# A two-layer diffusion trunk: vectors on ScalarE's queue, inputs loaded first, and the first projection's four jobs in two half passes

## The reference

```python
silu_c = jax.nn.silu(c)
sh1, sc1, g1, sh2, sc2, g2 = jnp.split((silu_c @ ada_w[i] + ada_b[i])[:, None, :], 6, axis=-1)
hl = modulate(rms_norm(x, norm1_g[i]), sh1, sc1)      # h * (1 + scale) + shift
q, k, v = jnp.split(h @ w_qkv, 3, axis=-1)            # w_qkv is 1024 x 3072
```

## Time and profile before

| | |
|---|---|
| median of 3 runs | 1165.8 us (1165.01 to 1168.77) |
| span of the profiled execution | 1166.4 us (no other time is given for it) |
| mean granted TensorE clock | 0.943 of full |
| TensorE busy | 983.8 us, 84% of the span |
| VectorE, ScalarE, GpSimd busy | 402.4, 365.3, 218.6 us |
| DMA | 321.76 MB, mean 276 GB/s |
| chain that ended last, by engine | PE 66%, DMA 18%, DVE 6%, issue 4%, ACT 3% |

### The profile page before, as it was taken

One profiled execution on the slowest core, in us unless ns is written; L12 is line 12 of the kernel. 1 busy time (PEld: TensorE's weight loads), 2 busy tenths in 40 slices (PEclk: granted clock), 3 DMA queues, 4 the chain that ended last, 5 costly groups with the idle time before them and its releaser, 6 DMA issues.

```text
span 1166.4 us, 24481 instructions
## 1 busy us (share of the span) xinstructions
PE 983.8 (84%) x9634; PEld 662.7 (57%) x9635; DVE 402.4 (34%) x848; ACT 365.3 (31%) x777; POOL 218.6 (19%) x329
## 2 busy tenths in 40 slices
PE   4899999988899979799898659999999768996571
PEld 1577777544555655466566447887555644664340
DVE  1533331346733522122122283122853621221113
ACT  3532222466832222122222344233751211120101
POOL 0000000000000034244344201910000132442221
PEclk9899999999999999899999879999999898998895
DMA  9766655998230759999999467224527789999983
GB/s 338 276 225 223 224 214 175 338 362 324 112 137 36 251 205 396 422 422 422 422 425 393 168 226 174 75 72 138 224 83 308 301 355 419 404 421 425 424 358 115
DMA packets 92967, 321.76 MB, mean 276 GB/s; under 512 B 21289, under 2 KB 33234, under 8 KB 80610
## 3 DMA queue, kind: packets, MB, share of 16 engines
q1 hardware_dynamic: 85026, 305.00, 67.9%
q0 software_dynamic: 7008, 12.62, 2.9%
q10 hardware_dynamic: 864, 3.15, 0.7%
HBM read 313.28 MB, written 13.99 MB: 281 GB/s over the span
## 4 chain that ended last, share of the span: by engine, by line
PE 66%; DMA 18%; DVE 6%; issue 4%; ACT 3%; SPq 1%; POOL 1%; POOLq 0%; DVEq 0%; ACTq 0%
PE ps L1953 22%; PE ps L1719 21%; DMA expert_sets<-in_moe_w_up_dram 10%; PE ps L1874 7%; PE ps L1616 5%; PE ps L1640 4%; DMA expert_sets<-in_moe_w_down_dram 3%; DMA ring<-in_ada_w_dram 2%; PE ps L1774 1%; PE ps L1801 1%; DMA ada_late<-in_ada_w_dram 1%; PE ps L1830 1%; DMA expert_rows<-moe,scatter_idx 1%; DMA val<-expert_rows 1%; PE ps L1657 1%
## 5 line engine op out<-in xcount | busy, mean ns | idle before, releaser
L1953 PE MATMUL ps<-expert_sets,moe 128*32 128x256 f32 x6304 | 366.7, 392 | 79.3 <-DMA expert_sets<-in_moe_w_up_dram 37.0
L1953 PEld LDWEIGHTS ps<-expert_sets,moe 128*32 128x32 f32 x6304 | 241.4, 113 | 203.3 <-issue 97.2
L1543 DVE STREAM_TRANSPOSE moe<-moe 128x256 f32<-128x256 f32 x70 | 45.8, 654 | 313.9 <-PE ps L1953 284.2
L1719 PE MATMUL ps<-w_high,x_high 128*128 128x512 f32 x352 | 142.0, 404 | 6.5 <-DVE x_low L490 5.1
L1719 PE MATMUL ps<-w_low,x_high 128*128 128x512 f32 x352 | 138.6, 394 | 0.0
L1719 PE MATMUL ps<-w_high,x_low 128*128 128x512 f32 x352 | 138.5, 393 | 0.0
L1092 ACT ACTIVATE moe<-ps 128x128 f32<-128x128 f32 x68 | 18.9, 278 | 318.5 <-PE ps L1953 309.4
L477 DVE TENSOR_TENSOR w_low<-ring,w_high 128x2048 fp32r<-128x2048 f32 x24 | 55.5, 2321 | 134.7 <-ACT w_high L474 134.7
L760 POOL MEMSET moe<- 128x128 f32 x2 | 0.4, 205 | 539.3 <-PE ps L1900 539.3
L784 POOL DMA_INDIRECT expert_rows<-moe,scatter_idx x74 | 76.0, 1027 | 85.6 <-POOL scatter_idx L821 41.4
L1719 PEld LDWEIGHTS ps<-w_high,x_high 128*128 128x128 f32 x352 | 66.7, 189 | 30.3 <-issue 14.7
(11 more groups left out here) (245 smaller groups left out, 1089.5 us busy)
## 6 DMA issues: line engine op xcount, KB each, us to landing
expert_sets<-in_moe_w_down_dram SPq DMA_DIRECT2D x32, 2048.0 KB
expert_sets<-in_moe_w_gate_dram SPq DMA_DIRECT2D x30, 2048.0 KB
expert_sets<-in_moe_w_up_dram SPq DMA_DIRECT2D x30, 2048.0 KB
ring<-in_ada_w_dram SPq DMA_DIRECT2D x16, 2048.0 KB, 8.1
ring<-in_diff_w_qkv_dram SPq DMA_DIRECT2D x6, 2048.0 KB, 8.7
ada_late<-in_ada_w_dram SPq DMA_DIRECT2D x6, 2048.0 KB, 12.4
ring<-in_na_w_qkv_dram SPq DMA_DIRECT2D x6, 2048.0 KB, 8.7
val<-expert_rows SPq DMA_DIRECT2D x12, 512.0 KB, 4.6
```

The costliest lines, as they stand in the source:

```text
L1543: dve.transpose(blk_inT, blk_in[b].rearrange("p (j k) -> p k j", k=KC)).then_inc(m_xt[l], 1)
L1719: mm = pe.matmul(ps[:, n % 2], x_part[:, k, tok], w_part, start=(k == 0 and i == 0), stop=(k == KC - 1 and i == 2))
L1953: mm = pe.matmul(ps[g * SLOTS:(g + 1) * SLOTS, bank, 0:n_out], lhs_T[:, k, :], weights(k, g), start=(k == 0), stop=(k == n_chunks - 1), sk ...
```

## The change

Seven parts.

1. The seven small loads are issued by ScalarE instead of SyncE, the constants last. SyncE begins with the two inputs.
2. SyncE's order is then modulation strips 0 and 2, weight strip 0 in two DMAs of 1 MB (chunks 0 to 3 with a semaphore of its own, `s_first_half`, and 4 to 7), modulation strips 1 and 3, the late vectors, strip 4. The slots of strips 0 to 4 stay. `place(a)` is a strip's place in this order, which all the counts of products, copies, turns and sums now use.
3. `first_modulation(half)` takes the place of `modulation(0, 0, 2)`: bias and gain for four chunks, once after strips 0 and 2 and once after 1 and 3, in three steps each. `s_mod` counts one more.
4. `stream_half` is half of `stream_in`; layer 0 uses it for both streams' first half, then for both streams' second half. The order of the input halves in layer 0 is `s + 2 * half`.
5. The first four jobs (all of weight strip 0) run in two half passes (`qkv_half`) of 12 matmuls into banks 0 to 3, one each; the context stream's turns use banks 4 and 5 instead.
6. TensorE's list for the opening is written out: 8 keep-busy products instead of none before strip 0, 5 before and 5 after the context stream's second turns (bank 1). The first half passes stand around the products of strips 1 and 3, and the second half passes in the loop, where the products of strips 4, 5, ... follow as before.
7. The last norm uses `s_ms` and `s_rt` instead of its own semaphores.

The diff, cut to its core:

```diff
+        FIRST_STRIPS = (0, 2, 1, 3)
+        EARLY_JOBS = TILES
+        def place(a):
+            return FIRST_STRIPS.index(a) if a < ADA_QKV else a
...
-                for a, slot in enumerate((KT_STRIP, VAL_STRIP, 2, 1)):
-                    add_ada(a, slot)
+                add_ada(0, KT_STRIP)
+                add_ada(2, 2)
                 add_qkv(0, 0)
+                add_ada(1, VAL_STRIP)
+                add_ada(3, 1)
                 add_ada(ADA_QKV, 1)
...
-                wait_strip(eng, l, st)
+                if l == 0 and p == 0 and half == 0:
+                    eng.wait_ge(s_first_half, 16)
+                else:
+                    wait_strip(eng, l, st)
...
+        STREAM_BANKS = [[(4, 5, 4, 5), (2, 3, 6, 7)], [(0, 1, 2, 3), (2, 3, 6, 7)]]
+        def job_bank(l, n):
+            return n if l == 0 and n < EARLY_JOBS else n % 2
...
 (SyncE)
-            small(cst[:], consts)
...
-            for j in range(2):
-                load_strip(0, j)
             sp.dma_start(resid[:, 0:CTX_TILES], ctx...).then_inc(s_x, 16)
             sp.dma_start(resid[:, CTX_TILES:TILES], x...).then_inc(s_x, 16)
-            for j in range(2, ADA_QKV + 1):
+            for j in range(2):
+                load_strip(0, j)
+            first_weights = diff_w_qkv[0].rearrange("(k p) n -> p k n", p=P)
+            sp.dma_start(strip(0, 2)[:, 0:KC // 2], first_weights[:, 0:KC // 2, 0:STRIP]).then_inc(s_first_half, 16)
+            sp.dma_start(strip(0, 2)[:, KC // 2:KC], first_weights[:, KC // 2:KC, 0:STRIP]).then_inc(s_ld[0], 16)
+            for j in range(3, ADA_QKV + 1):
                 load_strip(0, j)
...
 (ScalarE)
+            small(vec_rows[8:16, :], c...)
...
+            small(cst[:], consts)
...
-            for a in range(ADA_QKV // 2):
-                copy_mod(a)
             act.wait_ge(s_x, 32)
             for t in range(TILES):
                 norm1(0, t)
-            for a in range(ADA_QKV // 2, ADA_QKV):
-                copy_mod(a)
+            for i in range(ADA_QKV // 2):
+                copy_mod(i)
...
+                    split_weights(act, 0, 0, 0)
+                    act.wait_ge(s_mod, 1)
+                    for s in range(2):
+                        stream_half(act, 0, s, 0)
+                    split_weights(act, 0, 0, 1)
+                    for i in range(ADA_QKV // 2, ADA_QKV):
+                        copy_mod(i)
+                    act.wait_ge(s_mod, 2)
+                    for s in range(2):
+                        stream_half(act, 0, s, 1)
...
 (VectorE)
+                    for a in FIRST_STRIPS[:2]:
                         sum_mod(a)
-                    modulation(0, 0, 2)
+                    first_modulation(0)
+                    stream_half(dve, 0, 0, 0)
+                    split_weights(dve, 0, 0, 0)
+                    split_inputs(dve, 0, 0, 0)
+                    stream_half(dve, 0, 1, 0)
+                    split_inputs(dve, 0, 1, 0)
+                    split_weights(dve, 0, 0, 1)
+                    for a in FIRST_STRIPS[2:]:
+                        sum_mod(a)
+                    first_modulation(1)
+                    for s in range(2):
+                        stream_half(dve, 0, s, 1)
+                        split_inputs(dve, 0, s, 1)
...
 (TensorE)
+                if l == 0:
+                    keep_busy(8)
+                    mod_products(0)
+                    mod_turn(0)
+                    for s in range(2):
+                        pe.wait_ge(s_xn[0], CTX_TILES * (s + 1))
+                        turn_stream(s, (0, 1))
+                    mod_products(2)
+                    mod_turn(2)
+                    keep_busy(5, bank=1)
+                    copied_half(0)
+                    turn_stream(0, (2, 3))
+                    keep_busy(5, bank=1)
+                    qkv_half(0, 0)
+                    mod_products(1)
+                    qkv_half(1, 0)
+                    mod_turn(1)
+                    mod_products(3)
+                    mod_turn(3)
+                    qkv_half(2, 0)
+                    qkv_half(3, 0)
+                    pe.wait_ge(s_adr, ADA_QKV)
+                    turn_stream(1, (2, 3))
...
+                    for half in range(2):
+                        if half == 1 or l == 1 or n >= EARLY_JOBS:
+                            qkv_half(n, half)
```

More of the change, by code:

```diff
@@ L395, in add_ada @@
             def add_ada(a, slot):
-                add("ada", a, (ada_w[a // ADA], a % ADA, s_ada, a + 1), slot)
+                add("ada", a, (ada_w[a // ADA], a % ADA, s_ada, place(a) + 1), slot)
             def add_qkv(g, slot):
@@ L932, in _ @@
                             dst = tm(l, 0)[:, (m % 2) * STRIP:(m % 2 + 1) * STRIP]
[L933 removed]
+                        act.activation(dst, ps[:, job_bank(l, n)], ACT.Copy,
                                        scale=SCALE if g < 2 else 1.0).then_inc(s_qeA[l], 1)
@@ L1165, in modulation, with first_modulation @@
                         step(stt(m, m, 1.0, g, ALU.add, ALU.mult))
+                dve.sem_inc(s_mod, 1)
+            def first_modulation(half):
+                b = adab[:, 0:2 * KC].rearrange("p (i k) -> p i k", k=KC)
+                m = mod[:, 0, 0:2 * KC, :].rearrange("p (i k) s -> p i k s", k=KC)
+                ks = slice(half * KC // 2, (half + 1) * KC // 2)
+                for i in range(2):
+                    step(tt(m[:, i, ks], m[:, i, ks], b[:, i, ks].unsqueeze(2).to_broadcast([P, KC // 2, 2]), ALU.add))
+                g = vec[:, 16 + half * KC // 2:16 + (half + 1) * KC // 2].unsqueeze(2).to_broadcast([P, KC // 2, 2])
+                step(stt(m[:, 1, ks], m[:, 1, ks], 1.0, g, ALU.add, ALU.mult))
                 dve.sem_inc(s_mod, 1)
@@ L1678, in turn_stream, with copied_half @@
                         mm.then_inc(s_ht[l][s], 1)
+                def copied_half(number):
+                    for copied in (s_heA, s_heD):
+                        pe.wait_ge(copied[l], (number + 1) * KC // 4)
                 def turn_qk(n):
@@ L1723, in _ @@
-                    mm.then_inc(s_qm[l], 1)
+                    if half == 0 and is_last:
+                        mm.then_inc(s_half, 1)
+                    if half == 1:
+                        mm.then_inc(s_qm[l], 1)
+                if l == 0:
[21 more added lines that the diff above has]
+                    turn_stream(1, (2, 3))
+                else:
+                    pe.wait_ge(s_xn[1], CTX_TILES)
+                    turn_stream(0)
+                    copied_half(1)
@@ new lines, in _ @@
+                for n, (g, t) in enumerate(qkv_jobs[l]):
+                    if l == 1 and n == CTX_TILES:
+                        pe.wait_ge(s_xn[1], 2 * CTX_TILES)
+                        turn_stream(1)
+                    before = job_before_in_bank(l, n)
+                    if before is not None:
+                        kind, copied, value = qkv_copy[l][before]
+                        pe.wait_ge(copied, value)
+                    for half in range(2):
+                        if half == 1 or l == 1 or n >= EARLY_JOBS:
+                            qkv_half(n, half)
```

154 lines of the change are left out of this document (64 added, 90 removed).

## The result

The changed kernel takes 1158.24 us (median of 7, 1154.54 to 1159.45), the kernel before 1165.01 (median of 7, 1159.98 to 1168.77). The ratio is 0.993, with an interval of 0.9911 to 0.995: faster by 0.7%, and by 6.8 us between the medians. The interval corresponds to 5.8 to 10.4 us. The forecast was 1158.8.

The account below looks back on a forecast made before the run. The opening was held by the one DMA stream on SyncE's queue, then TensorE's own pace. Terms along TensorE's order put job 4 at 69.2 against 76.20, 7.0 less: 1158.8 against the median, range 1155.7 to 1164.0.

Parts of the forecast that it names:

- The gauge: Start of job 4 on TensorE: forecast at 69.2 against 76.20, everything behind it moving forward equally.
- the sum: Opening's terms added along TensorE's order up to job 4 at 69.2: 7.0 less, 1158.8 against the median.
- Rival C: Later stages: a load timed by something other than TensorE takes the gain back; 1165 to 1166, 6%.
- room until about 14.4: Opening: the small vectors could land until about 14.4 at no cost; each microsecond past that costs one.
- strip 0's products near 16, long form: Opening sign on TensorE: first strip's products start at their landing, 16.0, and take 3.64 after idleness.
- conditioning ready before 10: Opening sign: conditioning, ready 1.6 after the vectors land, would be there before 10.
- VectorE's chain: Behind strip 2: copies 0.95, low weights 2.25 and low inputs 1.23 set job 0's start at 31.8.
- Rival D: Opening: vectors on ScalarE's queue starve beside SyncE's full one; at worst landing at 37, giving 1181.4; 7%.
- Rival A: Opening: TensorE's clock stays low over turns and strip 2's products, adding 3.8: 1162.6; 12%.
- The new wait: Before job 3: strip 5 reuses slot 1, lands at 63.6, while TensorE is ready at 61.8.
- Rival B: Slot 1's loads set the pace: strips 4 and 5 land after 12.2, strip 5 4.9 later; 1163.7; 10%.
- Strip 0's landing: Opening loads: first modulation strip lands at 16.0, between an early bound of 15.5 and a late one of 17.0.

Follow-up runs that it names:

- e6: Changed kernel with the constants issued by SyncE behind strip 2 instead of by ScalarE; median 1168.01 us, ratio 1.0017 to the kernel before.
- e1: Changed kernel without the eight keep-busy products ahead of strip 0's products; median 1157.7 us (kernel before 1167.23).
- e7: Changed kernel with the constants on SyncE ahead of the inputs and strip 5 loaded into val's space; median 1157.86 us (kernel before 1166.75).
- e5: Changed kernel with 30 turns in place of the eight keep-busy products ahead of strip 0; 1163.35 us, one run.
- e2: Changed kernel with the constants issued by SyncE ahead of the inputs, six small vectors still by ScalarE; median 1157.38 us, ratio 0.9915 to the kernel before.

## Why the prediction was right

| step | forecast | measured |
|---|---|---|
| latent inputs landed | 10.8 | 9.0 |
| strip 0 landed | 16.0 | 15.25 |
| strip 0's products, start and end | 16.0, 19.6 | 18.62, 20.54 |
| strip 2's products | 22.9 | 23.58 |
| job 0, first half | 31.8 | 32.30 |
| second halves | 50.2 | 50.59 |
| strip 5 landed | 63.6 | 63.35 |
| job 4 | 69.2 | 69.14 |
| time | 1158.8 | 1158.24 |

**The gauge was right.** Job 4's start moved by 7.06, the sum had 7.0, and the median by 6.8. e6 shows the passage in the other direction: 9.9 later at job 4, 8.4 to 10 in the time. Rival C (the later stages take it back) is out as a whole, since the interval of the gain begins at 5.8; a part of 1 or so could not be seen beside the later stages' spread.

**One step failed and another hid it.** The sum let strip 0's products start at their landing, with "room until about 14.4" for the vectors. There was no such room. I had left out that the eight keep-busy products, which the change puts ahead of strip 0, stand behind the conditioning in TensorE's own list, and I had costed only the ten later ones. Conditioning 1.4 after the first turn and 6.7 of products before 15.25 mean that the vectors are on the path from a first turn at 7.2 on (8.6 where the products take 5.21), and it came at 10.59. That is a loss of 3.4 against the landing. But the same products gave strip 0's the short form, 1.92 instead of the 3.64 of the sum, so that the end was 0.9 late, not 3.4; e1 shows both sides of that trade. An error of 2.6 and one of 1.7 met, and 0.5 was left at job 0. That they met was luck: the sum had neither. Two signs of the prediction failed with this step, "strip 0's products near 16, long form" and "conditioning ready before 10": the conditioning was ready just before 12.01.

Behind strip 2 the sum named VectorE's chain as the path (31.8) and let TensorE's own list, ten keep-busy products and eight turns, end at 31.5 at no cost. In the trace the two tie: VectorE's low inputs end at 31.02 + 1.22 = 32.24, TensorE's list at 32.28, and the chain names the list.

**Rival D** (the vectors starve) had its mechanism right in part. ScalarE's queue did get the smaller share. Of the traffic from 5.0 to 10.5, by queue (q1 is SyncE's, q10 ScalarE's; packets, MB, share of the engines' time):

```profile
q1 hardware_dynamic: 599, 1.72, 79.5%
q10 hardware_dynamic: 338, 0.47, 23.8%
```

ScalarE's queue moved 0.47 of 2.19 MB, 21%, in 338 of the 937 packets, though both queues had work nearly all the time. The price of the vectors was one to one, as stated and as e6 and e7 show, but from 7.2 and not from 14.4.

**Rival A** (clock) did not come, because of the eight products; without them it comes in part (e1: 1.6 on the turns, nothing on strip 2's products). In e5 turns alone were ahead of products in the short form. The Trainium skill, TensorE: Matmul & The Clock Gate, Part 4, says that transposes do not count as busy in the same way and that the full clock does not engage for them; this one profile of float32 turns contradicts that.

**The new wait** for strip 5 was there, 1.1 instead of the 1.8 of the sum, as the load took 8.1 and not 8.7. This took back the 0.5 by which TensorE was late until then: a third error, small, that helped the number. **Rival B** was out: strips 4 and 5 landed after 8.0 and 8.1. **Strip 0's landing**, 15.25, lay just outside the bounds of 15.5 to 17.0; no run tells why, and nothing hung on it, as the products started later.

## What to carry to other kernels

Before costing a moved load, list what stands between its first user and the path on that engine: here warming products that looked like filler were 6.7 us of an in-order list. Small loads on a second queue came late beside a full one. Moving the constants ahead on the full queue brought the first turn forward by 1.7 and no more, as six small loads stayed behind on the other; moving all seven ahead of the inputs was not run. To remove a wait for a load, look at when the stream last stood still, not only at the buffer of the late load itself.

## What was not expected of the hardware

Two queues with work did not share the stream evenly: ScalarE's got 21% of the bytes, and in e2 its last load, 48 KB in rows of 512 bytes, was issued at 2.90 and released the first turn at 8.88, though only about 70 KB were on that queue. In the kernel before, with one queue and nothing ahead but the other small loads, the same load took from 3.07 to 5.03.

The moment at which TensorE comes up to speed varies between executions: the same eight products, behind long idleness, took 5.21 to 6.78 in nine profiles, and 3.62 where they followed other work. Read one by one in the changed kernel, their records last 634 ns up to those that begin near 17.3, and 379 ns at the end. The granted-clock column does not show this in the first 25 us: it reads 1.00 in every window from 12 to 18 of the changed kernel, and in e1's from 20 to 24, where sixteen turns take 3.53 instead of 1.91. There the durations have to be read.
